# Thirty-two modulation units of a fp32 transformer kernel: the two multiply-and-sum instructions of each become two jobs in successive steps of a hand-made plan

## What is computed

```python
c_act = silu(c)                                        # (1, 1024)
for layer in range(2):
    mod = c_act @ w_ada[layer] + b_ada[layer]          # (1, 3072): shift, scale, gate
    h = rms(x) * gain * (1 + scale) + shift
    y = gated_delta(h) if layer == 0 else stick(h, kv)
    x = x + gate * y
mkv = c_act @ w_ada_kv + b_ada_kv                      # (1, 2048): shift, scale of the kv norm
```

## Time and profile before

| what | us |
|---|---|
| three executions | 905.27, 906.47, 913.07 |
| their median | 906.47 |
| the profiled execution's own time | 904.68 |
| its span, first to last instruction | 902.9 |

### The profile page before, as it was taken

The page is one execution under the profiler, slowest core; times in us unless marked ns, Lnnn a source line. Parts: engine busy times, 40 slices in busy tenths (PEclk is TensorE's granted clock), DMA queues, the critical chain, the costliest instruction groups (busy, mean ns, idle before and its releaser), DMA issues.

```text
span 902.9 us, 16845 instructions
## 1 busy us (share of the span) xinstructions
PE 809.1 (90%) x7040; PEld 748.9 (83%) x7040; DVE 641.8 (71%) x1292; ACT 497.7 (55%) x1013; POOL 0.2 (0%) x4
## 2 busy tenths in 40 slices
PE   3988999989999999999978788888987879999988
PEld 3877988989899999999967677777776868978888
DVE  5477977897687888977868677666654888645464
ACT  4566644454556566664455635454662447566862
POOL 0000000000000000000000000000000000000000
PEclk9999999999999999999999899999996979999999
DMA  9522853766455667547762422212213456732211
GB/s 344 225 84 75 295 219 140 279 233 226 148 187 171 212 214 235 199 148 281 265 237 92 142 75 68 75 68 80 109 52 136 159 186 229 265 141 94 94 48 48
DMA packets 22684, 148.50 MB, mean 164 GB/s; under 512 B 2640, under 2 KB 3024, under 8 KB 6480
## 3 DMA queue, kind: packets, MB, share of 16 engines
q1 hardware_dynamic: 22608, 147.43, 45.9%
HBM read 146.37 MB, written 1.05 MB: 163 GB/s over the span
## 4 chain that ended last, share of the span: by engine, by line
PE 62%; DVE 24%; ACT 12%; issue 2%; DMA 0%; DVEq 0%; SPq 0%; ACTq 0%
PE ps L1952 48%; DVE wlo L1457 5%; DVE raw L1479 3%; DVE qT L1454 1%; DVE vt L1454 1%; DVE kT L1454 1%; DVE p0lo L1457 1%; ACT L1040 1%; DVE tmp L1454 1%; ACT whi L1061 1%; PE pp L2125 1%; PE pp L2287 1%; PE pp L2166 1%; PE pp L2298 1%; DVE Tm L1454 1%
## 5 line engine op out<-in xcount | busy, mean ns | idle before, releaser
L1952 PE MATMUL ps<-p0hi,whi 128*128 128x256 f32 x1128 | 329.8, 292 | 17.9 <-DVE p0lo L1457 7.7
L1952 PE MATMUL ps<-p0lo,whi 128*128 128x256 f32 x1128 | 318.2, 282 | 0.0
L1952 PE MATMUL ps<-p0hi,wlo 128*128 128x256 f32 x1128 | 317.9, 282 | 0.0
L1457 DVE TENSOR_TENSOR wlo<-raw,whi 128x512 fp32r<-128x512 f32 (+2 forms) x436 | 271.8, 659 | 25.7 <-ACT whi L1061 25.4
L1952 PEld LDWEIGHTS ps<-p0hi,whi 128*128 128x128 f32 x1128 | 215.0, 191 | 30.3 <-issue 18.9
L1061 ACT ACTIVATE whi<-raw 128x512 fp32r<-128x512 f32 (+2 forms) x436 | 237.9, 599 | 2.1 <-DMA raw<-wst 2.1
L1952 PEld LDWEIGHTS ps<-p0lo,whi 128*128 128x128 f32 x1128 | 215.5, 191 | 0.9 <-issue 0.7
L1952 PEld LDWEIGHTS ps<-p0hi,wlo 128*128 128x128 f32 x1128 | 215.2, 191 | 0.0
L1479 DVE CUSTOM_DVE_ANT_0 raw<-raw,cact,vc 128x1024 f32<-128x1024 f32 x64 | 79.5, 1278 | 0.0
L1952 PE MATMUL ps<-zhi,whi 128*128 128x256 f32 x176 | 49.5, 281 | 2.7 <-DVE wlo L1457 2.7
L1952 PE MATMUL ps<-zlo,whi 128*128 128x256 f32 x176 | 49.0, 279 | 0.0
(11 more groups left out here) (340 smaller groups left out, 1363.3 us busy)
## 6 DMA issues: line engine op xcount, KB each, us to landing
raw<-wst SPq DMA_DIRECT2D x125, 1024.0 KB, 5.0
raw<-wsd SPq DMA_DIRECT2D x16, 704.0 KB, 4.5
x<-xT SPq DMA_DIRECT2D x4, 256.0 KB, 4.9
m_x<-memT SPq DMA_DIRECT2D x1, 1024.0 KB, 8.2
outT<-x SPq DMA_DIRECT2D x4, 256.0 KB, 2.3
cact<-cB SPq DMA_DIRECT2D x1, 512.0 KB, 13.9
cst<-con SPq DMA_DIRECT2D x1, 356.0 KB, 12.2
smo<-conr SPq DMA_DIRECT2D x1, 320.0 KB, 11.8
```

The source lines that it names most:

```text
L1457: return v.tensor_tensor(lo, src, hi.bitcast(F32), ALU.subtract)
L1952: ins = t.matmul(o, a, b, start=first and q == 0, stop=last and q == len(ops) - 1, skip_group_check=True)
```

## The change

An "ada" job becomes (k, m), with m = 0 or 1, one instruction each. `prep_unit` puts both on `carried`, and `step()`, which takes one entry, emits the first in the step in which both stood before and the second in the step after it. The buffer counts as free, and all that waited for the pair waits, after the second.

```diff
     def prep_unit(self):
         k = self.prep
         if is_ada(self.units[k]):
-            self.carried.append(k)
+            self.carried += [(k, 0), (k, 1)]
             self.prep += 1
             return
...
     def ada_part(self):
-        k = self.carried.pop(0)
-        self.add("ada", k)
-        self.loaded_free.add(k)
-        self.load_units()
+        k, m = self.carried.pop(0)
+        self.add("ada", k, m)
+        if m:
+            self.loaded_free.add(k)
+            self.load_units()
...
                     if is_ada(units[k - NRAW]):
-                        e.wait_ge(*on("ada", k - NRAW))
+                        e.wait_ge(*on("ada", k - NRAW, 1))
...
                 elif kind == "ada":
-                    k, = i
+                    k, m = i
...
-                    for m in range(2):
-                        r = raw[k % NRAW][:, m * D:(m + 1) * D]
-                        c = col + 2 * n + m
-                        ins = v.tensor_tensor_reduce(out=r, in0=r, in1=cact[:, :], scale=1.0, scalar=V(bname, 2 * n + m), op0=ALU.mult,
-                                                     op1=ALU.add, accum_out=mod[:, c:c + 1])
-                    ins.then_inc(*tick("ada"))
+                    r = raw[k % NRAW][:, m * D:(m + 1) * D]
+                    c = col + 2 * n + m
+                    v.tensor_tensor_reduce(out=r, in0=r, in1=cact[:, :], scale=1.0, scalar=V(bname, 2 * n + m), op0=ALU.mult,
+                                           op1=ALU.add, accum_out=mod[:, c:c + 1]).then_inc(*tick("ada"))
```

More of the change, by code:

```diff
@@ L1606, in _ @@
                     if name == "outa":
-                        e.wait_ge(*on("ada", at("ada0", 11)))
+                        e.wait_ge(*on("ada", at("ada0", 11), 1))
                         for m in range(2):
@@ L1617, in _ @@
                     e.wait_ge(*unit_done("outb", n))
-                    e.wait_ge(*on("ada", at("ada1", 11)))
+                    e.wait_ge(*on("ada", at("ada1", 11), 1))
                     for m in range(2):
@@ L1655, in _ @@
                     col, gain, last = {"a": (8, "g_a", ("ada0", 7)), "kv": (56, "g_kv", ("adakv", 7)), "b": (32, "g_b", ("ada1", 7))}[site]
-                    e.wait_ge(*on("ada", at(*last)))
+                    e.wait_ge(*on("ada", at(*last), 1))
                     m = mod[:, col:col + 8]
```

## The result

| what | us |
|---|---|
| before, eight executions beside it | 909.98 median, 905.27 to 913.07 |
| after, eight executions | 904.5 median, 899.83 to 905.4 |
| ratio | 0.9936, 95% interval 0.9907 to 0.9965 |
| profiled execution after: own time, span | 902.12, 900.3 |

The kernel is 0.6% faster, 5.5 us by the medians. Forecast were 902.8 us, in a range of 898.5 to 907.5 us, and no difference beyond 1%; both held. But the forecast was worked from a profiled execution of 904.68 us and from three executions whose median was 906.47 us; the eight that ran beside the changed kernel have 909.98. As a difference it was 2.8 us, so the working has to be held against the ratios and the traces, not against the time alone.

What follows compares the result with a forecast made beforehand. TensorE was taken to set the time (busy 809.1 of 902.9 us), VectorE mattering only where TensorE waits for it. From the profiled 904.68 us, minus 3.4 gained plus 0.6 lost gave 901.9; predicted 902.8 us, range 898.5 to 907.5.

Steps and rivals of the forecast that it cites:

- The direction and the class: Whole kernel: slightly faster, 902.8 us, well below the 1% a measurement tells; chance of staying within 1% 0.89.
- Places where TensorE waits for the first lo: Down projection's first and third pair gain 0.6 us each, a part less a lo; first output projection 0.97; sum 2.2 us.
- Jobs that come earlier: Jobs between the steps start earlier: mLSTM's second and third head gain 0.80 us, delta rule's mask 0.35; sum 1.15 us.
- Sums on VectorE: Where VectorE's sum decides, gains are waited again: second-layer output projection keeps 0.1 us, query projection and 495 us 0.
- the wait of 4.15 us: Sign of being right, end of second-layer output projection: this wait grows by 0.5 to 1 us while 1.45 and 0.89 shrink.
- The second half in a chain: Second half enters a chain: 0.2 us lost at `Um` near 652 us, 0.4 at the head norm behind `f_m`; 0.6 in all.
- Transfers: Buffers come free later; ScalarE's unit wait at 101.57 us would have its load start 0.9 us later; cost 0.
- a sign against me: Sign of being wrong: a new ScalarE wait for a transfer near 102 to 110 us.
- Each wait goes whole: Rival: every wait behind a pair vanishes whole, the second part not waiting; 9.1 us gained, 895.6 us; chance 0.07.
- Nothing stays: Rival: each gain is waited again where VectorE's sum or ScalarE decides; 904.7 us, or 905.5; chance 0.13.
- The second half delays the generators: Rival: five pairs in generator chains cost the full price, 6.0 us against gains of 3.4; 907.3 us; chance 0.12.
- The clock, the fourth: Rival: one granted-clock fall around TensorE's long waits more or less is 1.8 us; two give 905.5 or 898.3; chance 0.08.

Runs made afterwards that it cites:

- two_apart: The changed kernel with the second half two steps behind the first instead of one, for all 32 pairs; ratio to the kernel before 0.9937.
- again: The changed kernel as it is, timed once more; ratio to the kernel before 0.9948, profiled execution 904.29 us.
- after_beside: The changed kernel as it is, timed once more beside the two kernels with moved pairs; ratio to the kernel before 0.9958.
- gain_places: Only seven of 32 pairs split (mLSTM heads 2 and 3, first output projection, down projection, delta rule at 675 us); ratio to the kernel before 0.9968.
- chain_places: Only the five pairs split whose second half falls into a generator's chain (two cross attention, 644, 744, 791 us); ratio to the kernel before 1.0007.
- rest_places: Only the other twenty pairs split, twelve at waits or in generator chains left whole; ratio to the kernel before 0.9983.
- moved_pairs: Kernel before, every pair still one job, six pairs moved from the second-layer output projection and down projection to the up projection; ratio 0.9964.
- delta_two: Kernel before with only the two pairs of the delta rule's last chunk split (644 and 675 us); ratio 1.0006.

## Why the prediction was right, and where it was off

**The direction and the class.** Right: a gain below what one measurement tells. The sum in the trace is -3.5 us against -2.8 predicted, the three ratios say -4.8 us, with -2.9 us for the seven pairs alone.

**Places where TensorE waits for the first lo.** Right, also in the form: "a part less a lo". 0.73 and 0.59 us for two terms of 0.6, and two_apart shows the remainder by removing it.

**Jobs that come earlier.** Right in place, undersized in the mLSTM: 1.42 us for 0.80. The step that failed is reading a printed wait as its price. Matmuls that run unhindered start 0.12 us apart, but the record of the last one before a wait is 0.28 us long and counts as busy, so a standstill is 0.16 us longer than printed; and the first one behind it holds the next up by 0.11 us more than the others do in the mLSTM and the down projection (0.23 us in place of 0.12 in the latter), by 0.08 in the output projection. A closed wait is worth its print and 0.24 to 0.27 us: 0.39 + 0.41 + 2 x 0.27 = 1.34 us. In the first output projection the starts give 0.72 and 0.68 us for the waits of 0.49 and 0.48, and 0.22 for a third one of 0.03 us at 172 us, which my sum left out. Of these 1.62 us 0.36 comes back near 188.6 us, where after has waits of 0.09 us, and 0.12 by the pace. PE of after at the third head, which started at 150.43 us:

```profile
149.74 0.59 PE L2089 MATMUL pp<-tr,cst 128*128 128x256 f32 x2
```

At the mask of 675 us the wait of 0.35 us went as predicted. That the size did too, -0.36 us by 681 us, is partly luck: the part ahead ran at the lower level as a whole in after, and from its fourth matmul on before. again, after_beside and gain_places have -0.24 to -0.27 us, and chain_places, where this pair is not split, has -0.37 by the clock alone.

**Sums on VectorE.** Right: 0.02 us in the query projection, 0.06 in the output projection. One sign was wrong: the wait of 4.15 us did not grow by 0.5 to 1 us, it is 4.09. The waits of 1.45 and 0.89 us shrank to 0.24 and 0.23, but what they gave was waited again inside the stage, in three new waits of 0.05 to 0.07 us and one of 0.51 us ahead of the last unit, so nothing was left for the norm's sum to take in. The wait of 3.02 us at 503 us did take in what was won ahead of it: 3.90 us.

```profile
504.40 2.08 PE L2133 MATMUL pp<-tr,cst 128*128 128x512 f32 x2 [3.90 <-ACT tr L1352]
```

By the rule of the Trainium skill, "TensorE: Matmul & The Clock Gate", section "HAM oscillation — how this bites in real kernels", the longer wait would have cost clock as well. Over 500 to 515 us the mean granted clock is 0.77 in both traces, so here it did not; and over 500 to 526 us it is 0.87 behind a wait of 3.02 us (before) and of 3.90 us (after), but 0.80 behind one of 3.05 us (chain_places). That the other wait when shortened to 2.55 us gave clock back (0.64 to 0.76 over the 14 us behind it) agrees with the rule.

**The second half in a chain.** Right. At 652 us the second half stands behind a lo and ahead of `Um`:

```profile
651.20 1.28 DVE L1479 CUSTOM_DVE_ANT_0 raw<-raw,cact,vc 128x1024 f32<-128x1024 f32 x1
...
652.40 0.41 DVE L1845 TENSOR_SCALAR Um<-pp 64x256 f32<-64x256 f32 x1
```

```profile
652.87 0.71 PE L2213 MATMUL pp<-vb,Um 128*128 128x128 f32 x4
```

TensorE was 1.76 us ahead; 654.40 - 1.76 = 652.64, so it starts 0.23 us late for 0.2 predicted. At 748 us `f_m` is 1.2 us later against the norm, as said, and the whole stage to 762 us loses 0.40 us as predicted, but not in the wait that I named: that is 0.99 us as before. Some 0.2 us of it is the clock by 743 us. The rest is a new wait of 0.12 us at 753.89 us, and it costs 0.2 us in after and 0.24 or 0.25 in again, after_beside, chain_places and two_apart; gain_places, rest_places and moved_pairs, where this pair is whole, lose nothing over 752 to 762 us. So the term of 0.4 us measured 0.25, and that it came out by the table is luck.

```profile
748.12 0.16 DVE L1455 SCALAR_TENSOR_TENSOR mod<-mod,vc 128x8 f32<-128x8 f32 x1
```

```profile
756.53 1.12 PE L2264 MATMUL ps<-tr,cst 128*128 128x512 f32 x2 [0.99 <-ACT tr L1417]
```

**Transfers.** Right in cost, short in size. ScalarE's wait for a unit was to grow by 0.9 us and grew by 2.3, and it costs TensorE nothing, since VectorE was behind. Why 2.3 and not 0.9 stays open:

```profile
104.06 2.19 ACT L1062 ACTIVATE whi<-raw 128x512 fp32r<-128x512 f32 x4 [4.38 <-DMA raw<-wst]
```

I had listed a new wait here as a sign against me. The old one grew instead, and it would have been a bad sign to name: this engine had the time.

**The rivals.** "Each wait goes whole" is out by the waits of 0.22 and 0.35 us that after keeps in the down projection, and by two_apart, which takes them away. "Nothing stays" is out by gain_places (0.9948 to 0.9987). "The second half delays the generators" is out by chain_places as to its size: 0.3 and 0.25 us at its places, in its own trace and in after's, against 6. The clock, the fourth, was a real term in both directions, more than its 0.08 allowed: -1.1 us by 690 us in the seven traces with every pair split and whole, -0.8 in chain_places, +3.8 us over 510 to 518 us in chain_places and delta_two. It came from execution to execution and not with the change.

## What to carry to other kernels

Splitting a long filler instruction pair paid here only where the engine that sets the time stood still within a step behind it: the traces have nearly all of the gain at 7 of 32 places, while the times (0.9968 for the seven, 0.9947 for all) leave room for a small worth of the others. Before spreading filler finer, look for stages where the helper engine's sum sets the end and move filler out of them altogether. With the split that gave 0.9905 and, with the rest, 0.9858, where the split alone gave 0.995; the moves without the split gave 0.9964. And price a wait of the main engine by the distance of the starts around it, not by the printed idle time.

## What the runs showed of the hardware

Unhindered 128x256 matmuls of the same stage do not keep one pace. The chain of work over 280 to 300 us, without a wait in either kernel (start, us, what), before and then after:

```profile
279.90 20.18 PE ps L1952 x173
```

```profile
279.99 20.02 PE ps L1951 x170
```

20.18/173 = 0.1166 us and 20.02/170 = 0.1178 us, at a granted clock of 1.00 in both. Taken from the starts, two levels near 0.1167 and 0.1178 us occur in every trace, and a shorter pace near 0.1135 us in most, for 10 to 50 us. The upper two hold for stretches of 10 us and more, in after the longer one nearly all the way from 157 us on; which stretch has which differs from one execution to the next. The +1.14 us of 203 to 404 us is mostly this (some 1100 matmuls x 0.0011 = 1.2 us), and TensorE counts as busy in it. Over 7040 matmuls the distance between the upper two is 7040 x 0.0011 = 7.7 us, nearly as much as the executions of one kernel scatter (904.38 to 913.88 for 35 of before). A single profile therefore cannot tell a difference of a few us by its span; only changes at one place can be read from it.

The granted clock takes its falls at other places in other executions of almost the same program: over 510 to 650 us its mean is 0.98 in before, after, gain_places and rest_places, and 0.94 in delta_two and chain_places, where the matmuls that before has at 516 to 517 us start 0.21 us apart and not 0.12. TensorE loses 4.0 us in this stretch in delta_two although its idle time is not longer (14.7 against 15.95 us). Up to 644 us its pairs are those of before.
